# Differential-attention scores from split queries and keys instead of fp32 products, in a two-layer trunk

## The reference, cut to what matters

```python
q1, q2, k1, k2, vc = _diff_qkv(p_lat[..., s2:], rope_diff)
k1_all = jnp.concatenate([k1c, k1], axis=1)          # context and latent keys
k2_all = jnp.concatenate([k2c, k2], axis=1)
scale_c = DIFF_DIM ** -0.5
# for each block of 128 queries:
p1 = jax.nn.softmax(jnp.einsum('bqhd,bkhd->bhqk', q1, k1).astype(F32) * scale, axis=-1)
p2 = jax.nn.softmax(jnp.einsum('bqhd,bkhd->bhqk', q2, k2).astype(F32) * scale, axis=-1)
return jnp.einsum('bhqk,bkhd->bqhd', (p1 - lam * p2).astype(v.dtype), v)
```

## Time and profile before

| | us |
|---|---|
| median of 3 runs | 2944.63 (2944.26 to 2946.18) |
| the profiled execution | 2947.07 |
| its span, first to last instruction | 2945.3 |
| PE busy in the span | 2863.0 (97%) |
| DVE busy | 1661.3 (56%) |
| ACT busy | 888.9 (30%) |
| mean granted clock of TensorE | 0.990 |
| first to last start of the differential scores (L914), both layers | 830.2 to 2480.6 |

### The profile page before, as it was taken

How to read it: one execution, slowest core, us unless ns; L and a number is a source line. 1 busy time by engine, 2 the same in 40 slices (tenths; PEclk the granted TensorE clock), 3 DMA queues, 4 the chain that set the end, 5 groups by cost and what they waited for, 6 DMA issues and landing times.

```text
span 2945.3 us, 43800 instructions
## 1 busy us (share of the span) xinstructions
PE 2863.0 (97%) x16930; PEld 2456.5 (83%) x16930; DVE 1661.3 (56%) x3097; ACT 888.9 (30%) x1390; POOL 106.7 (4%) x82
## 2 busy tenths in 40 slices
PE   6999999999999999999999999999999999999998
PEld 4888888888756888888888888888888767898996
DVE  5876677733466577767776335433443366543443
ACT  4221122223256442211222221122233255422222
POOL 0000000043000000000000000000023000000000
PEclk8999999999999999999999999999999999999999
DMA  6444344322300034433432213222222300233232
GB/s 224 134 124 127 93 133 128 103 63 58 81 1 1 29 97 136 125 121 108 126 120 89 64 57 116 70 64 59 69 71 67 80 1 1 81 91 100 86 103 68
DMA packets 422759, 255.39 MB, mean 87 GB/s; under 512 B 26017, under 2 KB 418057, under 8 KB 422666
## 3 DMA queue, kind: packets, MB, share of 16 engines
q1 hardware_dynamic: 422160, 254.00, 28.9%
q10 hardware_dynamic: 506, 0.13, 0.0%
HBM read 252.01 MB, written 2.10 MB: 86 GB/s over the span
## 4 chain that ended last, share of the span: by engine, by line
PE 93%; DVE 3%; ACT 2%; issue 1%; DMA 0%; SPq 0%; DVEq 0%; ACTq 0%
PE pair L694 56%; PE pair L688 26%; PE pair L914 2%; PE pair L962 2%; PE pair L648 2%; PE pair L930 1%; PE pair L939 1%; PE pair L890 1%; ACT buf L1246 1%; PE pair L947 1%; PE pair L872 1%; DVE lo_w L1381 0%; PE pair L878 0%; PE pair L883 0%; ACT hi_w L1045 0%
## 5 line engine op out<-in xcount | busy, mean ns | idle before, releaser
L694 PE MATMUL pair<-n_hi,hi_w 128*128 128x260 f32 (+2 forms) x3456 | 847.5, 325 | 17.0 <-DVE n_lo L1420 10.7
L694 PE MATMUL pair<-n_lo,hi_w 128*128 128x256 f32 (+1 forms) x3456 | 845.4, 325 | 0.0
L694 PE MATMUL pair<-n_hi,lo_w 128*128 128x258 f32 (+2 forms) x3456 | 844.7, 325 | 0.0
L694 PEld LDWEIGHTS pair<-n_hi,hi_w 128*128 128x128 f32 x3456 | 532.1, 189 | 80.6 <-issue 11.0
L694 PEld LDWEIGHTS pair<-n_hi,lo_w 128*128 128x128 f32 x3456 | 537.0, 190 | 58.5
L694 PEld LDWEIGHTS pair<-n_lo,hi_w 128*128 128x128 f32 x3456 | 535.0, 189 | 54.8
L1381 DVE TENSOR_TENSOR lo_w<-raw_w,hi_w 128x1024 fp32r<-128x1024 f32 (+1 forms) x296 | 394.6, 1333 | 302.2 <-ACT hi_w L1045 301.5
L1045 ACT CAST hi_w<-raw_w 128x1024 fp32r<-128x1024 f32 (+1 forms) x296 | 328.9, 1111 | 653.8 <-PE pair L694 365.8
L1553 DVE SCALAR_TENSOR_TENSOR mod_acc<-mod_w,silu_c,mod_acc 128x256 f32<-128x256 f32 x896 | 364.7, 479 | 0.0
L1476 DVE TENSOR_TENSOR buf<-pair,rstd 128x512 f32<-128x512 f32 (+1 forms) x308 | 164.9, 571 | 308.7 <-PE pair L694 308.6
L688 PE MATMUL pair<-h_hi,hi_w 128*128 128x512 f32 x1232 | 338.8, 345 | 0.0
(11 more groups left out here) (185 smaller groups left out, 2009.8 us busy)
## 6 DMA issues: line engine op xcount, KB each, us to landing
raw_w<-in_ffn_w SPq DMA_DIRECT2D x176, 512.0 KB, 3.8
mod_w<-in_w_mod SPq DMA_DIRECT2D x64, 1024.0 KB, 5.1
raw_w<-in_ffn_w SPq DMA_DIRECT2D x64, 704.0 KB, 4.7
raw_w<-in_w_in SPq DMA_DIRECT2D x38, 512.0 KB, 3.9
raw_w<-in_w_out SPq DMA_DIRECT2D x16, 512.0 KB, 4.0
pro_scale<-in_w_mod SPq DMA_DIRECT2D x2, 2048.0 KB, 15.4
pro_shift<-in_w_mod SPq DMA_DIRECT2D x2, 2048.0 KB, 13.4
x_tok<-in_x SPq DMA_DIRECT2D x4, 512.0 KB, 5.3
```

The lines of the kernel that those rows point to most:

```text
L694: mm = pe.matmul(pair[s][:, a:a + m], wt[:, k * P:(k + 1) * P], src[:, of(k):of(k) + m], start=opens, stop=closes)
```

## The change

The differential queries and keys get a high part of type float32r and a low part, and `scores_diff` adds three products (high by high, high by low, low by high) in place of one fp32 product. ACT makes the high parts (`high_dqk`), DVE the low parts (`low_dqk`); each waits for the other through the new semaphores `dqk_hi` and `dqk_lo`, and PE waits for `dqk_lo` in `scores_diff`. The eight tiles of a layer are numbered j = 0 to 7 in the order query, key of head 0, query, key of head 1, and so on. For j = 0 to 3 the split stands among the tasks: ACT after `("v", 3)` and the three `vm`, DVE after the rotations of `T_DK`, `T_DQ+1`, `T_DK+1` and `T_DQ+2`. For j = 4 to 7 it stands at the end of turns 1 to 4, behind `exponential(c, 2)` on ACT and behind `combine_diff(c)` on DVE. Keys have 768 columns; queries have 768 in layer 0 and 512 in layer 1. The high parts go to tiles that are free at that time, the low parts in place of the originals. The other attention, MLA, keeps its fp32 products.

```diff
--- before.py
+++ after.py
@@ -156,6 +156,7 @@
     return sum(1 for task in TASKS[:count] if task[2] == who)
 
 
+DQK_AFTER = [("v", 3), ("vm", 0), ("vm", 1), ("vm", 2)]
 N_ACT, N_DVE = read_out("a", len(TASKS)), read_out("d", len(TASKS))
 N_STEPS = [len(steps_of(i)) for i in range(DEPTH)]
 N_PIECES = [len(pieces_of(i)) for i in range(DEPTH)]
@@ -226,6 +227,7 @@
         exp_sum = sb("exp_sum", 3 * N_SLOT)
         inv_sum = sb("inv_sum", 3 * N_SLOT)
         sub_sum = sb("sub_sum", max(N_STEPS))
+        rstd_r, = overlay(("rstd_r", TOK, F32R))
         rstd = sb("rstd", TOK)
 
 
@@ -253,6 +255,7 @@
         n_hi = sb("n_hi", N_COLS, F32R)
         n_lo = sb("n_lo", N_COLS, F32R)
 
+        proj_r, = overlay(("proj_r", T_IN * TOK, F32R))
         proj, v_mla = overlay(("proj", T_IN * TOK, F32), ("v_mla", (TOK // P) * 256, F32))
         x_tok, pro_shift, c_rows, rows, lam_row, silu_wide = overlay(
             ("x_tok", (TOK // P) * D, F32), ("pro_shift", KD * D, F32), ("c_rows", P, F32), ("rows", 3 * P, F32),
@@ -339,6 +342,8 @@
         exp_done = [sem(f"exp_done{s}") for s in range(3)]
         p_diff = sem("p_diff")
         inv_mla = sem("inv_mla")
+        dqk_hi = sem("dqk_hi")
+        dqk_lo = sem("dqk_lo")
         t_diff = sem("t_diff")
         t_mla = sem("t_mla")
         pt_diff = sem("pt_diff")
@@ -433,6 +438,22 @@
             return slice(i, i + 1)
 
         turned = pair[2][:, TOK:1024]
+
+        def dqk_tile(j, tensor=proj):
+
+            return tile(tensor, (T_DQ, T_DK)[j % 2] + j // 2)
+
+        def dqk_hi_tile(j):
+
+            if j < 4:
+                return n_lo[:, (KD // 2 + j) * TOK:(KD // 2 + j + 1) * TOK]
+            if j == 7:
+                return n_hi[:, 6 * TOK + 6 * MV:7 * TOK + 6 * MV]
+            return rstd_r[:, :] if j == 6 else tile(proj_r, T_POOL + j - 4)
+
+        def dqk_rope(j):
+
+            return TASKS.index(("rope", (T_DQ, T_DK)[j % 2] + j // 2, "d"))
 
         def acc_mla(L, c):
 
@@ -901,6 +922,7 @@
                 def scores_diff(c):
 
                     h, at, k0, nk = steps[c]
+                    pe.wait_ge(dqk_lo, 2 * (L * HEADS + h + 1))
                     for s in range(2):
                         if st0 + c:
                             pe.wait_ge(exp_done[s], st0 + c)
@@ -909,12 +931,14 @@
                             pe.wait_ge(o_mla, st0 + c - 2)
                         if a and c >= 2:
                             pe.wait_ge(o_diff, st0 + c - 1)
-                        for s in range(2):
-                            rows_s = slice(DDIM * s, DDIM * (s + 1))
-                            mm = pe.matmul(pair[s][:, a:a + m], tile(proj, T_DQ + h, P, at)[rows_s, :],
-                                           tile(proj, T_DK + h, m, k0 + a)[rows_s, :], start=True, stop=True)
-                            if a + m == nk:
-                                mm.then_inc(s_ready[s], 1)
+                        q, k = ([dqk_hi_tile(j), dqk_tile(j, proj_r)] for j in (2 * h, 2 * h + 1))
+                        for n, (i, j) in enumerate(((0, 0), (0, 1), (1, 0))):
+                            for s in range(2):
+                                rows_s = slice(DDIM * s, DDIM * (s + 1))
+                                mm = pe.matmul(pair[s][:, a:a + m], q[i][rows_s, at:at + P],
+                                               k[j][rows_s, k0 + a:k0 + a + m], start=(n == 0), stop=(n == 2))
+                                if a + m == nk and n == 2:
+                                    mm.then_inc(s_ready[s], 1)
 
                 def scores_mla(c):
 
@@ -1198,6 +1222,12 @@
                 if w["what"].endswith("_up"):
                     cnt["h"] += FG
 
+            def high_dqk(L, j):
+
+                n = TOK if j % 2 or L < DEPTH - 1 else SEQ
+                act.wait_ge(out_dve, L * N_DVE + read_out("d", dqk_rope(j) + 1))
+                act.copy(dqk_hi_tile(j)[:, 0:n], dqk_tile(j)[:, 0:n]).then_inc(dqk_hi, 1)
+
             def mixer(L):
                 w_last = [w for w in SWEEPS if w["layer"] == L and w["what"] == "in"][-1]
                 more = L < DEPTH - 1
@@ -1230,6 +1260,8 @@
                             ins = act.activation(of(2 * arg + e, m)[0:NOPE, :], src[NOPE * e:NOPE * (e + 1), 0:m],
                                                  ACT.Identity, scale=SC_MLA if what == "uq" else 1.0)
                     ins.then_inc(out_act, 1)
+                    if (what, arg) in DQK_AFTER:
+                        high_dqk(L, DQK_AFTER.index((what, arg)))
                     if what == "uq" and arg == 2:
 
                         act.wait_ge(out_dve, L * N_DVE + read_out("d", TASKS.index(("rope", T_KR, "d")) + 1))
@@ -1291,6 +1323,8 @@
                         if c:
                             act.wait_ge(t_mla, st0 + c)
                         exponential(c, 2)
+                    if 1 <= c <= 4:
+                        high_dqk(L, c + 3)
                 act.wait_ge(o_diff, st0 + n_steps)
                 act.activation(sub_sum[:, 0:n_steps], sub_sum[:, 0:n_steps], ACT.Ln, bias=eps_col[:, 0:1],
                                scale=1.0 / DIFF_V).then_inc(sub_ready, 1)
@@ -1654,6 +1688,13 @@
                         ins = dve.tensor_copy(mla_q(h, nq_all)[NOPE:, :], q_rot[h * ROPE:(h + 1) * ROPE, 0:nq_all])
                 ins.then_inc(out_dve, 1)
 
+            def low_dqk(L, j):
+
+                n = TOK if j % 2 or L < DEPTH - 1 else SEQ
+                dve.wait_ge(dqk_hi, 2 * HEADS * L + j + 1)
+                dve.tensor_tensor(dqk_tile(j, proj_r)[:, 0:n], dqk_tile(j)[:, 0:n],
+                                  dqk_hi_tile(j)[:, 0:n].bitcast(F32), ALU.subtract).then_inc(dqk_lo, 1)
+
             def mixer(L):
                 w_last = [w for w in SWEEPS if w["layer"] == L and w["what"] == "in"][-1]
                 more = L < DEPTH - 1
@@ -1680,6 +1721,9 @@
                         if arg == T_KR:
                             dve.wait_ge(tabm_full, 16 * 3 * (L + 1))
                         rotate(L, a, arg, nq_all)
+                        j = {T_DK: 0, T_DQ + 1: 1, T_DK + 1: 2, T_DQ + 2: 3}.get(arg)
+                        if j is not None:
+                            low_dqk(L, j)
 
                 steps, n_steps, st0 = steps_of(L), N_STEPS[L], sum(N_STEPS[:L])
                 pieces, pc0 = pieces_of(L), sum(N_PIECES[:L])
@@ -1733,6 +1777,8 @@
                     if c < n_steps:
                         maxima(c, 2)
                         combine_diff(c)
+                    if 1 <= c <= 4:
+                        low_dqk(L, c + 3)
 
                 def scale_diff(h):
 
```

## The result

| | before | after |
|---|---|---|
| median, us | 2945.40 (2944.26 to 2946.67, 4 runs) | 2972.11 (2966.15 to 2972.56, 4 runs) |
| profiled execution | 2947.07 | 2972.40 |
| its span | 2945.3 | 2970.6 |
| mean granted clock of TensorE | 0.990 | 0.984 |

The change costs 26.7 us: the ratio is 1.0086, with a 95% interval of 1.0073 to 1.0099. The prediction was 2955.6 with a range of 2947.5 to 2963.0: slower, as said, but well over twice as much, and outside the range.

The account below looks back on a forecast made before the run. PE (TensorE, 93% of the chain of waits) was taken to bound the long turns. Gains -6.2, waits +13.8 and clock +3.4 us sum to +11.0 on a median of 2944.6: 2955.6 us, range 2947.5 to 2963.

Parts of the forecast that it names:

- The scores: Split products on PE take 1.26 us in place of 1.49, saving 0.23 a long turn, -4.6 us over 20 turns.
- the three turns named as signs: The period of turns 6, 13 or layer 1's 10 was to be 6.99 us.
- The rival of the uncovered weight loads: In the scores, two more pairs of loads, 2 x 0.12, eat the 0.23, gains about 0: 2961.8 us, 5%.
- First turns: Faster scores save 0.6 us twice in turns 0 and 1 of layer 0, -1.2, and -0.4 in layer 1.
- The split among the tasks: Casts and subtractions for heads 0 and 1 among the tasks cost 0, with 0.5 us let into the range.
- The waits in turns 1 to 4: DVE waits for ACT's late cast, delaying the next maxima by 1.85 us (1.37 with 512 columns): +13.8 us in sum.
- The signs: Turns 1 to 4: periods of 8.1 to 9.1 us, DVE's subtraction waiting for ACT some 3 us, PE for ACT 2.2.
- The clock: Six PE gaps that long in the delayed turns: two falls of 1.7 us each, +3.4 (bounds 0 and five falls, 8.5).
- whether a gap is noticed hangs on its position: Reason given for taking only two clock falls, though six gaps of PE in the delayed turns are that long.

Follow-up runs that it names:

- experiment 9: Experiment 3 with the third product (low queries by high keys) left out of the scores, so part of the computation is missing: 2932.49 us.
- experiment 5: Changed kernel with one unused fp32 filler product behind the MLA scores of turns 2 to 5: 2966.45 us.
- experiment 1: Changed kernel with three unused fp32 filler products behind the MLA scores of turns 2 to 5, all waits kept: 2952.94 us.
- experiment 3: Changed kernel with ACT's cast in turns 1 to 4 moved ahead, to behind exponential(c, 1): 2939.31 us.
- experiments 2 and 3: Besides experiment 3, the second: changed kernel with DVE's subtraction of turn c moved behind combine_diff(c+1), ACT's cast left in place: 2939.87 us.
- experiment 8: Changed kernel with casts, subtractions and waits kept, but the fp32 scores of the kernel before and the parts unused: 2973.81 us.
- experiments 1 and 5 to 8: Besides experiment 1, experiment 5, experiment 7 and experiment 8, the sixth: changed kernel with two filler products in turns 2 to 5: 2956.73 us.
- experiment 7: Experiment 3 with only the last cast (key of head 3, turn 4) left at the changed kernel's place, behind exponential(4, 2): 2948.05 us.

## Why the prediction failed, step by step

**The scores: right.** 1.25 us against 1.26, and 6.97 to 6.99 against 6.99 for a long turn. The rows R6 to R23 and R6 to R15 of the table say -2.2 each, forecast -2.1. Two of the three turns named as signs were ill chosen: turn 6 has 6.99 us, but turn 13 has 6.51 and layer 1's turn 10 has 8.06, where before they had 6.76 and 8.31. The saving is the same there. The rate of the split product was not shown on half the rows by any row of before; taking it from the projections held (experiment 9). The rival of the uncovered weight loads is out. Six pairs of loads, each following products on the same half, fit into 1.25 us; the pairs of 512-column products, one on each half, start some 0.24 us apart and the pairs of 256 columns 0.115. The Trainium skill (TensorE: Matmul & The Clock Gate, Part 3, "What overlaps and what doesn't") has a load run beside a product only where the row groups differ; by that rule the trace disagrees.

**First turns: nearly right.** -2.1 against -1.2 in layer 0, of a time that differs by 3.1 us between executions of the same code, so the agreement is partly luck. In layer 1 it is +0.8 in place of -0.4. Of that, +0.7 arose between R23 of layer 0 and the end of PE's idle gap of 2.75 us ahead of layer 1's turns (1391.62 us against 1390.93), a stretch that took 1390.0 to 1392.2 in the other versions with the same tasks. From there to R1 it took 9.48 us against 9.39 before, with a low stretch of 10.2 us (2378.3 to 2388.5) and not the 6.8 of the earlier trace rows; with 6.8 us, in experiment 5, it took 8.90, about the saving that was forecast.

**The split among the tasks: right.** No cost shows there: the first scores of layer 0 start at 829.34, before the change at 830.18.

**The waits in turns 1 to 4: right, to a tenth.** With the clock held (experiment 1) they cost 7.1 and 6.1 us net of the faster scores, forecast 7.2 and 6.2. The signs came as told: DVE's subtraction waits for ACT (3.13 us behind turns 3 and 4 of experiment 1), and `values_mla` for the exponential by 2.1 us.

**The clock: wrong, and this is most of the miss.** The step that failed was "two falls, 1.7 us each, +3.4", with bounds of 0 and five falls. Measured were six. By the periods behind them (change less experiment 1) they cost 1.64, 1.62 and 2.72 us in layer 0 and 1.63, 2.84 and 3.20 in layer 1, 13.7 together, so 10.3 more than the term. Three of them lasted 6.8 us where I took half of 3.4 for all. The other part of the miss is the 4.1 us behind the turns. It too is time at the low clock. Low stretches of the kernel after from 2500 us on (columns as above; there are four, of which 2569.40:2576.20 has PE busy for 5.98 and the last, 1.80 long, for nothing), and below them one of experiment 3:

```profile
2511.40:2514.80 3.40, 3.40 (x18) 3.40 (x18) 0.59 (x2) 0.31 (x1) 0.00 (x0) 0.50 0.00 0
...
2955.20:2965.40 10.20, 5.55 (x26) 5.55 (x27) 4.59 (x7) 2.16 (x3) 0.00 (x0) 0.50 0.12 51
```

```profile
2922.30:2932.50 10.20, 5.79 (x27) 5.79 (x28) 4.36 (x7) 2.39 (x3) 0.00 (x0) 0.50 0.14 60
```

PE works at 1.2 GHz for 14.93 us in them, against 6.17 in those of the kernel before; half of the difference is 4.4. In experiment 1 they have the length of before again. But this is not shown to come of the waits: experiments 2 and 3, which have no gap in the turns, took 466.9 and 467.1 us from R15 to the end, against 464.3 before and 468.4 after. So these stretches differ between executions also where no turn is delayed, and why was not tried.

The reasoning behind the clock term failed in two places. I read the tolerance off one row, 1.87 us idle in 3.40 with the clock at 1.00 (last of the earlier trace rows), and treated 2.2 us as just beyond it. That row is one gap, with dense work on both sides:

```profile
2488.61 0.41 PE L662 MATMUL pair<-ident,proj 128*128 128x128 f32 x2 [1.87 <-ACT buf L1246]
```

```profile
2483.10:2486.50 3.40, 3.34 (x31) 3.36 (x30) 2.91 (x6) 1.50 (x5) 0.00 (x0) 1.00 0.00 0
2489.90:2493.30 3.40, 3.40 (x30) 3.36 (x30) 0.92 (x2) 1.17 (x5) 0.00 (x0) 1.00 0.01 2
```

The same gap stands in all twelve profiled executions, 1.87 or 1.88 us long, and in two of them, those of the change and of experiment 8, the clock fell behind it; the first low stretch above is that fall. One row in which the clock held was thus no tolerance: in the delayed turns 845.80:849.20 with 1.95 us idle was followed by a fall, and 2395.40:2398.80 with only 1.66 was too. And "whether a gap is noticed hangs on its position" was taken as one chance in three without a row for it. Nothing of before bounded the falls below all eight turns, or the cost of one below 3.4 us (half of a low stretch of 6.8), so that 27 us, not 8.5, was the upper end.

All gaps of the delayed turns, in the profiled executions of the change and experiments 1 and 5 to 8, by length:

| gap ahead of `values_mla` | falls behind it |
|---|---|
| 1.59 to 2.14 us | 20 of 21 |
| 1.20 to 1.41 us | 4 of 11 |
| 0.36 to 0.84 us | 0 of 10 |

So in these turns the ladder is steep between 0.8 and 1.6 us. Length alone does not decide, though. The gap of 1.87 us at the end of layer 1's turns was followed by a fall in 2 of 12 executions, and the two gaps of 1.24 to 1.44 us that each execution has in the short turns of layer 0 by none in 24. Open is what else decides: why 1.63 us (layer 0, turn 5 of the change) was let pass where 1.20 was not, and why nearly every gap of the delayed turns was answered where the one of 1.87 us mostly was not. The position of the gap in time, which the prediction named, remains a rival that no experiment moved by itself; experiment 7 shows only that no row of gaps is needed. Each kernel is counted in one execution only.

## What to carry over

An engine that is not the bottleneck, put to wait at the head of its queue for late work of a third, stops the bottleneck behind it; look for the latest place at which the operand is needed and the earliest at which its maker is free. Here moving the casts, or the subtractions, by up to a turn took the change from +0.9% to -0.2%. A stall of TensorE is to be priced with the clock behind it: with the clock held the waits cost 13.6 us (2952.94 of experiment 1 less 2939.31 of experiment 3), and with empty gaps 19.2 more (2972.11), of which 13.7 are seen to be falls of the clock right behind the gaps. Where such a gap can't be removed, filling it with products nobody reads gave those 13.7 back.

## What was not expected of the hardware

- The granted clock fell behind 20 of 21 gaps of 1.59 us or more in the delayed turns, also behind a single one, and behind 4 of 11 of 1.20 to 1.41 us; yet behind a gap of 1.87 us at the end of layer 1's turns it fell in 2 of 12 executions only. The low clock then lasts 3.4 or 6.8 us though PE has work through all of it.
- A filler product makes the kernel faster: three of them in eight turns bring 2972.11 us down to 2952.94.
- Split products of 64 rows each on the two halves of the array run side by side at the rate that the projections have on full rows: six of 512 and six of 256 columns in 1.25 us, with their entry and exit.
